# A state-space layer computed in 64 chunks of 8 tokens in place of a scan over all 512 tokens

## The reference, cut to what matters

```python
proj = _rmsnorm(h, norm_mix_g) @ w_in            # q, k, v, u: 512 columns each
bu_r = jnp.einsum('blgc,gpc->blgp', uf, bbr)     # and bu_i, 64 states p of each of 32 groups g
_, _, xr, xi = lax.associative_scan(_complex_affine_combine, (a_r, a_i, bu_r, bu_i), axis=1)
y = (jnp.einsum('blgp,gcp->blgc', xr, c_re) - jnp.einsum('blgp,gcp->blgc', xi, c_im) + d_skip * uf)
y = jax.nn.gelu(y.reshape(bsz, seq, 512), approximate=False)
y = y * jax.nn.sigmoid(y @ w_glu + b_glu)
```

## Time and profile before

| | us |
|---|---|
| median of 3 runs | 4976.72 (4976.24 to 4978.61) |
| the profiled execution, its own time | 4975.26 |
| its span | 4973.5 |
| busy PE, DVE, ACT, POOL | 4665.8, 2156.7, 1487.8, 1883.3 |
| mean granted TensorE clock | 0.969 |

### The profile page before, as it was taken

One profiled execution on the slowest core, in us unless ns is written; L12 is line 12 of the kernel. 1 busy time (PEld: TensorE's weight loads), 2 busy tenths in 40 slices (PEclk: granted clock), 3 DMA queues, 4 the chain that ended last, 5 costly groups with the idle time before them and its releaser, 6 DMA issues. The chain is left out here.

```text
span 4973.5 us, 51485 instructions
## 1 busy us (share of the span) xinstructions
PE 4665.8 (94%) x19788; PEld 3540.3 (71%) x19788; DVE 2156.7 (43%) x4436; ACT 1487.8 (30%) x2282; POOL 1883.3 (38%) x852
## 2 busy tenths in 40 slices
PE   7777899999999999999999989899999998888999
PEld 6226678888888788887887845678878874355887
DVE  8696347963332233333440252444134135654440
ACT  2313332334444211112222234332232232343321
POOL 3032334456665444444444400334444431012443
PEclk9798999999999999999999989999999999999999
DMA  3012223445545656565223200222222221012222
GB/s 115 26 34 72 85 69 112 134 144 182 176 165 182 201 183 191 185 193 163 89 96 99 91 19 18 81 77 94 94 93 93 97 81 43 17 49 66 89 93 85
DMA packets 212740, 519.23 MB, mean 104 GB/s; under 512 B 16912, under 2 KB 82704, under 8 KB 209680
## 3 DMA queue, kind: packets, MB, share of 16 engines
q1 hardware_dynamic: 128016, 448.82, 27.7%
q10 hardware_dynamic: 84480, 67.12, 4.3%
HBM read 446.66 MB, written 69.21 MB: 104 GB/s over the span
## 5 line engine op out<-in xcount | busy, mean ns | idle before, releaser
L187 POOL TENSOR_TENSOR ring_rounded<-ring,highs_rounded 128x1024 fp32r<-128x1024 f32 x687 | 1683.8, 2452 | 2732.5 <-ACT highs_rounded L181 2715.2
L385 PE MATMUL bank<-arena_rounded,ring_rounded 128*128 128x512 f32 (+1 forms) x4488 | 1783.3, 397 | 89.9 <-DVE hT_rounded L403 41.1
L387 PE MATMUL bank<-arena_rounded,highs_rounded 128*128 128x512 f32 (+1 forms) x4488 | 1781.1, 397 | 0.0
L181 ACT ACTIVATE highs_rounded<-ring 128x1024 fp32r<-128x1024 f32 x687 | 727.7, 1060 | 2052.4 <-PE bank L387 1610.4
L386 PE MATMUL bank<-hT_rounded,highs_rounded 128*128 128x512 f32 x3128 | 1229.5, 393 | 0.0
L385 PEld LDWEIGHTS bank<-arena_rounded,ring_rounded 128*128 128x128 f32 x4488 | 853.4, 190 | 282.2 <-issue 86.2
L387 PEld LDWEIGHTS bank<-arena_rounded,highs_rounded 128*128 128x128 f32 x4488 | 852.3, 190 | 198.5
L386 PE MATMUL bank<-arena_rounded,highs_rounded 128*128 128x512 f32 (+1 forms) x2112 | 822.7, 390 | 0.0
L386 PEld LDWEIGHTS bank<-hT_rounded,highs_rounded 128*128 128x128 f32 x3128 | 593.7, 190 | 141.5
L386 PEld LDWEIGHTS bank<-arena_rounded,highs_rounded 128*128 128x128 f32 x2112 | 401.6, 190 | 90.8
L1251 DVE TENSOR_TENSOR arena<-qT,arena 128x512 f32<-128x512 f32 x64 | 150.6, 2354 | 372.2 <-ACT qT L1216 371.6
(11 more groups left out here) (316 smaller groups left out, 4569.3 us busy)
## 6 DMA issues: line engine op xcount, KB each, us to landing
ring<-pages_in SPq DMA_DIRECT2D x687, 512.0 KB, 3.4
act_table<-arena SPq DMA_DIRECT2D x128, 256.0 KB, 4.0
gate_table<-qT SPq DMA_DIRECT2D x16, 2048.0 KB, 7.1
arena<-act_table ACTq DMA_DIRECT2D x128, 256.0 KB, 4.0
arena<-gate_table ACTq DMA_DIRECT2D x32, 1024.0 KB, 8.6
arena<-ssm_in SPq DMA_DIRECT2D x16, 256.0 KB, 2.6
arena<-mem_in SPq DMA_DIRECT2D x3, 1024.0 KB, 4.8
arena<-spread_in SPq DMA_DIRECT2D x5, 512.0 KB, 4.8
```

The lines of the kernel that those rows point to most:

```text
L181: nc.scalar.activation(f32r(page_high(p)), slot(p), ACT.Copy).then_inc(masked_pages.sem, 1)
L187: nc.gpsimd.tensor_tensor(f32r(slot(p)), slot(p), part_of(page_high(p)), ALU.subtract).then_inc(split_pages.sem, 1)
L385: low_last = nc.tensor.matmul(out, f32r(w_low), f32r(x_high), start=start, stop=False)
L387: return low_last, nc.tensor.matmul(out, f32r(w_high), f32r(x_high), start=False, stop=stop)
```

## The change

- The state-space layer is done right after block 2, in a new block (`state_chunks`), ahead of `head_norm` and `attention`. `ssm` is gone.
- The pages of `w_in` come in another order: u first, then q, k, v. The drain of u (`times_by_chunks`) writes it with the token's place in its chunk outermost.
- `turn_tables` makes other tables: powers of `a` up to 8, the chunk matrices `into` (8 powers times B) and `outof` (9 powers times C), each in steps of three DVE instructions of 128 x 512, and then cosines and sines for 64 chunks only. `upper_products` and `upper_halves` are gone. The estimated cost of an instruction is `0.25 + n * 1.6e-3`.
- u goes to a DRAM table and comes back as 8 DMAs with channel and place in the chunk on the partitions, in runs of 64 elements (256 bytes). One more DMA loads B and C (1 MB), one more the two constant matrices (`swap`, `same_group`).
- `state_chunks`: PE transposes `into` (16 quarters of 4), ACT copies them out of PSUM; in four batches of 8 groups PE multiplies, DVE turns and does one scan of 512 columns; then PE makes the lag matrices from `outof` and `into`, DVE turns the ends back and spreads the lags into block-diagonal matrices, and PE makes the outputs from the states and from the lags. The outputs from the states go to a second DRAM table and come back in 32 DMAs of 256-byte runs.
- The gelu moves into the gate `project`, after a DVE addition of the two parts; the four products of the gate move into the same block, behind each sigmoid.

```diff
+        groups = 32
+        chunk = 8
+        n_chunks = SEQ // chunk
...
+                sp.dma_start(params[:, 0:256], groups_dram).then_inc(groups_in, 16)
...
+            def cost(n):
+                return 0.25 + n * 1.6e-3
...
+            link.eng.wait_ge(ahead.sem, ahead.at(16))
+            a, b = wide(groups, 16)
+            for first, other, by_first, by_other, out, order in (
+                    (raw_b, other_b, in_re, in_im, into, [(7 - j, j) for j in range(8)]),
+                    (raw_c, other_c, power_re, power_im, outof, [(l, l) for l in range(9)])):
+                for l, at in order:
+                    link(nc.vector.tensor_tensor(a, first, by_first[:, l, :][:, :, None].broadcast_to([P, groups, 16]),
+                                                 ALU.mult))
+                    yield cost(512)
+                    link(nc.vector.tensor_tensor(b, other, by_other[:, l, :][:, :, None].broadcast_to([P, groups, 16]),
+                                                 ALU.mult))
+                    yield cost(512)
+                    link(nc.vector.tensor_tensor(out[:, :, at, :], a, b, ALU.add))
+                    yield cost(512)
+            link.eng.sem_inc(tables_made.sem, 1)
...
+            while m < n_chunks:
+                w = min(groups, 512 // m)
+                for g in range(0, groups, w):
+                    c_, s_ = cosines[:, g:g + w], sines[:, g:g + w]
+                    by = [x[:, g:g + w][:, :, None].broadcast_to([P, w, m]) for x in (cos, sin)]
+                    yield from turn(c_[:, :, m:2 * m], s_[:, :, m:2 * m], c_[:, :, 0:m], s_[:, :, 0:m],
+                                    by[0], by[1], w, m)
                 m *= 2
-            link.eng.sem_inc(shifted.sem, 1)
+                if m < n_chunks:
+                    yield from double()
+            link(nc.vector.tensor_copy(rate, mag8[:, :, None].broadcast_to([P, groups, n_chunks])))
+            link(nc.vector.memset(rate[:, :, 0:1], 0.0))
...
+                    elif gelu is not None:
+                        for k in range(nk):
+                            act.wait_ge(made.sem, made.at(k + 1))
+                            rows = gelu[0](k).rearrange("p (j c) -> p c j", j=chunk)
+                            nc.scalar.activation(gelu[2](k).rearrange("p (c j) -> p c j", j=chunk), rows, ACT.Gelu)
+                            nc.scalar.activation(f32r(high(k)).rearrange("p (c j) -> p c j", j=chunk), rows,
+                                                 ACT.Gelu).then_inc(masked_h.sem, 1)
...
+                    if gated is not None:
+                        for b in range(uses):
+                            dve.wait_ge(free.sem, free.at(b + 1))
+                            nc.vector.tensor_tensor(gated[0](b), gated[0](b), gated[1](b), ALU.mult)
...
+        def state_chunks(uT):
...
+                    def load(b):
+                        sp.wait_ge(y_kept[b].sem, y_kept[b].at(16))
+                        for g in range(batch):
+                            sp.dma_start(y_rows[16 * g:16 * g + 16, b, :].rearrange("p (i n) -> p i n", i=chunk),
+                                         y_dram[:, :, batch * b + g, :].rearrange("i o n -> o i n")).then_inc(y_in.sem, 16)
+                    for b in range(batches):
+                        sp.wait_ge(copied.sem, copied.at(b + 1))
+                        sp.dma_start(y_dram[:, :, batch * b:batch * b + batch, :].rearrange("i o g n -> (i o) g n"),
+                                     by_group(y_chunks[:, b, :])).then_inc(y_kept[b].sem, 16)
+                        if b >= 1:
+                            load(b - 1)
+                    load(batches - 1)
...
+                    def turn(q):
+                        if q >= 2:
+                            pe.wait_ge(turned2.sem, turned2.at(q - 1))
+                        for g in range(4):
+                            last = nc.tensor.transpose(bank[q % 2][:, g * P:g * P + P],
+                                                       into[:, 4 * q + g].rearrange("p j c -> p (j c)"), mat(IDENT))
+                        last.then_inc(turned.sem, 1)
+                    def enter(b):
+                        pe.wait_ge(turned2.sem, turned2.at(2 * b + 2))
+                        if b == 0:
+                            pe.wait_ge(u_in.sem, u_in.at(16 * chunk))
+                        if b >= 2:
+                            pe.wait_ge(shifted.sem, shifted.at(b - 1))
+                        for part in range(2):
+                            for g in range(batch):
+                                last = nc.tensor.matmul(bank[2 + 2 * (b % 2) + part][:, n_chunks * g:n_chunks * g + n_chunks],
+                                                        turned_in[b][:, g, 64 * part:64 * part + P],
+                                                        chunks_in[:, batch * b + g, :], start=True, stop=True)
...
+                    def leave(b):
+                        pe.wait_ge(weighed.sem, weighed.at(b + 1))
+                        if b == 0:
+                            pe.wait_ge(drawn.sem, drawn.at(1))
+                        else:
+                            pe.wait_ge(copied.sem, copied.at(b))
+                        for g in range(batch):
+                            last = nc.tensor.matmul(bank[0][:, n_chunks * g:n_chunks * g + n_chunks],
+                                                    outof[:, batch * b + g, 1:9, :].rearrange("p l c -> p (l c)"),
+                                                    before[:, batch * b + g, :], start=True, stop=True)
+                        last.then_inc(summed.sem, 1)
+                    def inside(c):
+                        pe.wait_ge(paired.sem, paired.at(c + 1))
+                        pe.wait_ge(shifted.sem, shifted.at(batches))
+                        for l in range(chunk):
+                            m = SEQ - n_chunks * l
+                            last = nc.tensor.matmul(bank[2 + c][:, n_chunks * l:SEQ], within[c][:, l, :], uT(c)[:, 0:m],
+                                                    start=(l == 0), stop=(l == chunk - 1))
+                    for q in range(4):
+                        turn(q)
+                    for b in range(batches):
+                        enter(b)
+                        for q in range(2 * b + 4, min(2 * b + 6, 2 * batches)):
+                            turn(q)
+                    pe.wait_ge(turned2.sem, turned2.at(2 * batches))
+                    for g in range(groups):
+                        last = nc.tensor.matmul(bank[0][:, 16 * g:16 * g + 16],
+                                                outof[:, g, 0:8, :].rearrange("p l c -> p (l c)"), into[:, g, 7, :],
+                                                start=True, stop=True)
+                    last.then_inc(compared.sem, 1)
+                    swap_ends(0)
+                    pe.wait_ge(drawn.sem, drawn.at(1))
+                    for c in range(4):
+                        last = nc.tensor.transpose(bank[1][:, c * P:c * P + P], lags[:, c * P:c * P + P], mat(IDENT))
+                    last.then_inc(apart.sem, 1)
+                    swap_ends(1)
+                    for b in range(batches):
+                        leave(b)
+                        if b + 2 < batches:
+                            swap_ends(b + 2)
+                        inside(b)
...
+                        act.wait_ge(turned.sem, turned.at(q + 1))
+                        got = bank[q % 2][:].rearrange("p (g n) -> p g n", g=4)
+                        to = turned_in[q // 2][:, 4 * (q % 2):4 * (q % 2) + 4, :]
+                        nc.scalar.activation(to[:, :, 0:128], got, ACT.Copy)
+                        nc.scalar.activation(to[:, :, 128:192], got[:, :, 0:64], ACT.Copy).then_inc(turned2.sem, 1)
...
+                    def enter(b):
+                        dve.wait_ge(scored.sem, scored.at(b + 1))
+                        link(nc.vector.tensor_tensor(p0, by_group(bank[2 + 2 * (b % 2)][:]), cols_of(cosines, b), ALU.mult))
+                        link(nc.vector.tensor_tensor(p1, by_group(bank[3 + 2 * (b % 2)][:]), cols_of(sines, b), ALU.mult))
+                        dve.sem_inc(shifted.sem, 1)
+                        link(nc.vector.tensor_tensor(parts[0], parts[0], parts[1], ALU.add))
+                        at = arena[:, 16640 + 512 * b:17152 + 512 * b]
+                        link(nc.vector.tensor_tensor_scan(ends[b], at, parts[0], 0.0, ALU.mult, ALU.add))
+                        dve.sem_inc(exped.sem, 1)
+                    def leave(b):
+                        end = by_group(ends[b])[:, :, 0:n_chunks - 1]
+                        swapped = by_group(bank[6 + b % 2][:])[:, :, 0:n_chunks - 1]
+                        c, s = (cols_of(x, b)[:, :, 0:n_chunks - 1] for x in (cosines, sines))
+                        q0, q1 = (x[:, :, 0:n_chunks - 1] for x in (p0, p1))
+                        link(nc.vector.tensor_tensor(q0, end, c, ALU.mult))
```

(44 more changed lines are left out.)

374 lines of the change are left out of this document (159 added, 215 removed).

## The result

| | us |
|---|---|
| kernel before, median of 4 runs | 4976.48 (4970.06 to 4978.61) |
| changed kernel, median of 4 runs | 4907.81 (4903.86 to 4910.61) |
| ratio, 95% interval | 0.9863 (0.985 to 0.9877) |
| the profiled execution, its own time and span | 4905.1, 4903.0 |
| predicted | 4888 (4872 to 4912) |

The change takes 68.7 us off, 1.4%. The prediction had 88.6 us. Profiled against profiled it is 4975.26 - 4905.1 = 70.2 us, and the forecast for that pair was 4886.7, so 18.4 us are to be explained.

The account below looks back on a forecast made before the run. DVE was taken to set the pace in both the projection and `ssm`. 4975.3 + 52.4 (later `head_norm`) - 140.5 (`ssm` gone) - 0.5 (gate) = 4886.7, with 1.4 for the median 4888 us; range 4872 to 4912.

Parts of the forecast that it names:

- my upper bound: Loads of u: twice as many runs as `gate_table`, 17.2 us to landing, at 0.067 us a run per DMA engine.
- Rivals 2 and 4: 256-byte runs cost twice the upper bound, 4904 to 4908, chance 0.08; or 0.42 us each, slower than before, 0.02.
- (b): New block, four batches: DVE sets the pace at 3.43 us each, PE needs 3.3; the last reaches DVE at 18.8.
- (c): New block, PE's 32 lag products: 3.9 us, done at 22.7; with a copy and a swap 23.5.
- (d): New block, four batches back to outputs: DVE 3.45 us each, PE slightly slower, from 25.0 to 39.9.
- (e): New block's end: behind the last output's copy at 38.3 SP issues one store and 16 loads, 9.2 us, to 47.5.
- (a): New block's filling: PE's transposes and ACT's copies done at 4.6, 16 matmuls at half clock 3.9; DVE starts at 8.5.
- two gelus of the first part (the pair was 1.04): Gate's start: addition, these gelus and a subtraction come before PE, 3.3 us in place of 1.65, so 1.6 lost.
- Rival 1: PE stays at the lower clock in the new block: about +22 us, 4910; chance 0.14.
- rival 3 (a shorter block) and 5: New block 40 us and projection 3 less, 4876, chance 0.15; or new block as long as `ssm`, chance 0.01.
- My sign for rival 1: New block's later batches: eight products of 64 columns taking 1.9 us would show PE at the lower clock.
- My own case: The forecast of the whole kernel with its own range, 4878 to 4900 us; chance 0.60.

Follow-up runs that it names:

- the second profile: The changed kernel itself run once more, unedited: profiled execution 4913.3 us, median 4908.67 us, ratio 0.9861.

## Why the prediction was off, step by step

**The stages** were read rightly: `ssm` went whole (140.5 us), `head_norm` and `attention` kept their 108.3 us.

**The projection** was right in kind. VectorE has no wait, 14 of its instructions are stalled, the first drain came at 47.45 (forecast about 47), and the tables end at 146.6 (forecast 148.7): the stalls were 1.2 to 2.2 us each and 25 in all, where I had 29.1, and the copy at the end took 1.23 in place of 2.3. Moving the last doubling away moved the end by as much. TensorE finished at 124, not 131, because outputs 6 to 9 were drained at 86.7 to 101.4 (forecast 92 to 106); the 22.6 us from there were as forecast. That cost nothing: it only lengthened the idle time, 22.9 us.

**The way of u** was hidden, as forecast, with more to spare. SyncE's issues of it, with the time to landing:

```profile
L1997 SPq DMA_DIRECT2D qT<-u_table x8: 376/697/1148, 124.2 to 129.4; - x8
...
DMA to landing us min/median/max: 4.7/7.2/8.0
```

The last is issued at 129.4 and the slowest takes 8.0 us, so all is there by 137.4, 13 us before TensorE needs it (150.72). Per DMA engine there are 256 runs of 256 bytes, in at most 13.2 us: 0.052 us a run, against the 0.067 of my upper bound. Rivals 2 and 4 hung on that price and fell here. The Trainium skill, *DMA: Bandwidth & Descriptors*, Specifications, has transfers below 512 bytes read, modified and written; this trace shows no doubling of a run's price by it. The issues cost 0.70 us each (median), not 0.54, with nobody behind them.

**The new block** is where the prediction failed, and the step is the price of a product in (b), (c) and (d): "A matmul of one column takes 0.122 us, so those of 64 and 16 columns cost their weight load", and likewise 0.46 us for 512 columns of f32. Both numbers are right for a record, but a product of f32 operands is two records. The evidence stood in the earlier trace rows: TensorE has 192 records in `ssm`, while the code has 6 products in each of 16 turns. Point by point, from the block's start, forecast and measured: VectorE starts (8.5, 7.5); the last batch reaches it (18.8, 19.9); lag products done (22.7, 29.4; they took 3.9 and 9.8); first outputs begin (25.0, 33.7); a batch of outputs (3.4, 5.8 to 6.8); last output copied (38.3, 55.0); end (49, 64.3). The tail (e) was right: 9.3 us from the last copy, forecast 9.2. That (a) came out nearly right is luck: I had the first batch as 16 records at half the clock, 3.9 us, and it was 32 records at the full clock, 3.68; in the second profile it was 32 at half the clock, 6.93. The two terms for a batch in (d) were also rounded up, to 1.2 from 0.98 and to 2.2 from 2.07, which hid a little of the error.

With one record in place of two in most products, the block came out at 49.8 us, so the doubled count is enough to explain nearly all of the 15 us. A part of it overlaps with the clock: with wide lag products, which keep the clock up, the block is 4.4 us shorter at the same count (2.6 in the products, 1.0 in the two matmuls behind). At least 10 of the 14.4 us thus go only with the count.

The Trainium skill, *FP8 and Floating Point Precision*, TensorE Precision Notes, has full FP32 go through the array four times. The traces agree for wide operands: twice 0.46 us for 512 columns of f32 against 0.22 for rounded ones. For the 64-column products, which cost their weights, the factor measured is two.

**The gate** was forecast at -0.5 us and came out at +4.2. The failed step is "two gelus of the first part (the pair was 1.04)". The pair is 2.1 us, because its input is read at a stride of 64 elements, and TensorE then gets a part every 1.9 to 2.0 us instead of all at once. With the gelus in order TensorE began 3.3 us behind the block's start, which is what I had forecast. I had bounded the strided writes of VectorE in the projection (1.10 us for a drain, 0.69 for a plain one), and not ScalarE's reads. The Trainium skill, *SBUF — State Buffer*, Door 1, says that each access that crosses to another line of 16 bytes pays a penalty; 1.06 against 0.61 us agrees with it.

**The rivals.** Rival 1 was right in mechanism for some executions and wrong in size (8 us of 22); rival 3 (a shorter block) and 5 fell. My sign for rival 1 misled: eight products of 64 columns did take 1.95 us in the later batches, but at the full clock (1.00 from 190 to 206 us), as 16 records. What happened, a doubled record count, was none of the rivals. My own case, 4878 to 4900, missed the median by 8 us, and that the wide range held it is luck: it reached to 4912 only because rivals 1 and 2 had a price similar to that of the error.

## What to carry to other kernels

Count an engine's records against the instructions in the code before using one as a unit price: here 192 records for 96 products stood in the first group of rows. Count by kind of instruction, since the transposes were one record each. When work is moved into a block of its own, add up each engine in it; the longest sum, TensorE's 58.6 us, was the block, and the engine that sets the pace changes with the change. An idle engine at a block's end and another at the next block's start are one opportunity: moving 10 us of tables across the border won 10.95.
